# Second block: projections of unnormalised tokens ahead of the norm's root, and attention scores read from banks of their own

## The reference

```
mod = split(silu(c) @ w_mod + b_mod, 6)      # shift1, scale1, gate1, shift2, scale2, gate2: vectors
xn  = rms_norm(x, g1) * (1 + scale1) + shift1
p   = xn @ w_in                              # queries, keys, values, Fourier, convolution, pool
x   = x + gate1 * (concat(attention, fourier, conv, pool) @ w_out)
xn  = rms_norm(x, g2) * (1 + scale2) + shift2
x   = x + gate2 * ((silu(xn @ w_a) * (xn @ w_g)) @ w_ffn_out)
```

## Time and profile before

| | us |
|---|---|
| median of three runs | 2863.41 |
| span of the profiled execution, first to last instruction | 2801.5 |
| around the span (median less span) | 61.9 |
| TensorE busy in the span | 2548.0 |
| VectorE, ScalarE, GpSimd busy | 1445.6, 908.4, 1104.0 |

### The profile page before, as it was taken

How to read it: one execution, slowest core, us unless ns; L and a number is a source line. 1 busy time by engine, 2 the same in 40 slices (tenths; PEclk the granted TensorE clock), 3 DMA queues, 4 the chain that set the end, 5 groups by cost and what they waited for, 6 DMA issues and landing times.

```text
span 2801.5 us, 29890 instructions
## 1 busy us (share of the span) xinstructions
PE 2548.0 (91%) x9872; PEld 1720.8 (61%) x9872; DVE 1445.6 (52%) x3086; ACT 908.4 (32%) x2255; POOL 1104.0 (39%) x1163
## 2 busy tenths in 40 slices
PE   7899899987988888998998889998887999979999
PEld 6567655433434455686555546574365888857888
DVE  1732776898877436316767767777545100161000
ACT  1242254445553322422444445423333100132000
POOL 0000576676777600003776666766634000070000
PEclk9999999999999999999999999999998999989999
DMA  6465899999999963658999999999931344413444
GB/s 249 150 255 185 352 420 421 420 420 381 407 420 420 420 260 135 248 189 316 420 420 420 420 420 402 420 421 420 421 138 60 135 151 150 143 68 112 155 153 150
DMA packets 187329, 817.52 MB, mean 292 GB/s; under 512 B 20608, under 2 KB 22688, under 8 KB 154160
## 3 DMA queue, kind: packets, MB, share of 16 engines
q0 software_dynamic: 148816, 549.32, 48.1%
q1 hardware_dynamic: 38368, 266.35, 25.7%
HBM read 814.54 MB, written 1.05 MB: 291 GB/s over the span
## 4 chain that ended last, share of the span: by engine, by line
PE 50%; DMA 18%; POOL 13%; DVE 11%; issue 6%; ACT 1%; SPq 0%; ACTq 0%; DVEq 0%; POOLq 0%
PE work L642 42%; DMA arena<-experts_down,arena 10%; PE acc L642 7%; DMA arena<-experts_up,arena 7%; POOL arena L583 6%; POOL arena L610 6%; DVE arena L1754 3%; DVE arena L1669 1%; DMA ring<-stream 1%; DVE small L1592 1%; PE work L716 1%; DVE arena L1592 1%; DVE mx L1604 1%; DVE arena L1603 0%; DVE arena L1930 0%
## 5 line engine op out<-in xcount | busy, mean ns | idle before, releaser
L642 PE MATMUL acc<-arena 128*128 128x512 f32 x1868 | 892.7, 614 | 151.6 <-DMA arena<-experts_up,arena 106.9
L610 POOL DMA_INDIRECT arena<-experts_down,arena x512 | 495.6, 968 | 811.0 <-DVE arena L1738 570.7
L1754 DVE SCALAR_TENSOR_TENSOR arena<-arena,acc 128x1024 f32<-128x1024 f32 x512 | 619.1, 1220 | 329.6 <-DMA arena<-experts_down,arena 315.2
L642 PE MATMUL work<-arena,ring 128*128 128x256 f32 x3460 | 760.0, 382 | 19.5 <-ACT arena L1522 14.5
L642 PEld LDWEIGHTS work<-arena,ring 128*128 128x128 f32 x3460 | 660.8, 191 | 122.1 <-issue 24.6
L642 PEld LDWEIGHTS acc<-arena 128*128 128x128 f32 x1868 | 346.8, 194 | 602.3 <-issue 469.4
L583 POOL DMA_INDIRECT arena<-experts_up,arena x512 | 493.3, 963 | 199.9 <-issue 147.1
L642 PE MATMUL work<-h,ring 128*128 128x256 f32 (+1 forms) x1504 | 339.5, 380 | 8.4 <-DMA ring<-stream 6.0
L642 PEld LDWEIGHTS work<-h,ring 128*128 128x128 f32 x1504 | 279.5, 194 | 75.7 <-issue 40.1
L1310 ACT ACTIVATE arena<-arena 128x2 f32<-128x2 f32 x256 | 52.0, 203 | 598.8 <-DVE arena L1754 392.6
L642 PE MATMUL work<-lent,ring 128*128 128x256 f32 x992 | 224.3, 379 | 0.0
(11 more groups left out here) (241 smaller groups left out, 1833.5 us busy)
## 6 DMA issues: line engine op xcount, KB each, us to landing
ring<-stream SPq DMA_DIRECT2D x252, 1024.0 KB, 4.9
arena<-experts_down,arena POOLq DMA_INDIRECT x512, 14.7
arena<-experts_up,arena POOLq DMA_INDIRECT x512, 14.8
arena<-na_bias POOLq DMA_DIRECT2D x2, 2048.0 KB, 14.5
arena<-consts POOLq DMA_DIRECT2D x1, 2392.0 KB, 20.2
lent<-consts POOLq DMA_DIRECT2D x2, 1024.0 KB, 16.3
arena<-consts POOLq DMA_DIRECT2D x1, 1816.0 KB, 19.3
x<-x_in SPq DMA_DIRECT2D x1, 1024.0 KB, 5.7
```

The source lines that it names most:

```text
L610: pool.indirect_dma_start(down[:, (l * PICKS + n) % ROWS, :], None, experts[2 * l], bass.IndirectOffsetOnAxis(ap=expert[:, n:n + 1], axis=0))\
L642: ins = nc.tensor.matmul(o, w, r, start=start, stop=stop, **kw)
L1754: ins = v.scalar_tensor_tensor(row, row, 1.0, tok, ALU.mult, ALU.mult, accum_out=dot[:, n:n + 1])
```

## The change

Since the root is one factor for each token, it can be multiplied in behind a projection as well as ahead of it. The change does so for two of the projections behind each of the four norms. VectorE makes a second set of tiles, `gx2`: `x1` by the column `gs`, and beside the 256 tokens a 257th column that holds the shift. TensorE multiplies one projection of `gx2` ahead of the square sums and one behind them; in the result the first 256 columns want the root yet, and the 257th is the projected shift. VectorE reads that out (`scale_raw`): the column to `raw_bias`, the rest by the reciprocal root. Ahead of the mixers these are the two projections `a` of the convolution (ScalarE's copies of them are gone), ahead of the feed-forward the pair of the first hidden tile.

The square sums take three products instead of eight: VectorE adds the squares of the first six tiles (`add_square`), the last two go to TensorE as they are. The normalised tiles are now `gx2` by the reciprocal root. The scaling stands in `add_gated` behind each residual tile; in the first layer's first norm it stands by itself.

In the attention of the second block the scores go to the four banks of `acc` and not to `work`; VectorE takes the maximum there, ScalarE reads them there for the exponential, with the scale in it, and the pass L1603 is gone. TensorE waits, from the third pair on, for the exponentials of two pairs earlier. A number of semaphores of the first block, one for each layer before, become one for both with counts that go on; the order of work there stays. In the diff these lines are left out.

```diff
-            if kind in "STO":
+            if kind in "TO" or kind == "S" and beside:
...
+        gx2 = carve(KD, T + 2)
+        raw_bias = carve(2, 1)
...
+        def score_bank(u):
+            return acc[:, (u % 4) * 2 * T:(u % 4 + 1) * 2 * T]
...
+                    if kind == "S" and not beside:
+                        if p >= 2:
+                            pe.wait_ge(sem(f"{name}_exp"), pair[1] - 3)
+                        for u in pair:
+                            mm(score_bank(u), units[u]["q"][0], units[u]["k"], inc=sem("scored2"))
...
-                square_sum(f"norm2_{l}", f"sq2_{l}", k1("ones_d"), lambda k: h2[:, k, :], KD, T, 1)
-                for i in range(N_FM2):
+                def raw_group(item, norm):
+
+                    b = bank(item)
+                    for k in range(KD):
+                        w = tile()
+                        pe.wait_ge(sem("gx2"), (norm - 1) * KD + k + 1)
+                        mm(b[:, 0:T + 1], w, gx2[:, k, 0:T + 1], k == 0, k == KD - 1,
+                           inc=bank_full if k == KD - 1 else None)
+                        read()
...
+                def sum_of_squares(item, ready, norm):
+
+                    b = bank(item)
+                    pe.wait_ge(sem("sq_part2"), norm)
+                    mm(b[:, 0:T], k1("ones_d"), sq_part2, True, False)
+                    for k in (KD - 2, KD - 1):
+                        pe.wait_ge(sem(ready), k + 1)
+                        mm(b[:, 0:T], k1("ones_d"), h2[:, k, :], False, k == KD - 1,
+                           inc=bank_full if k == KD - 1 else None)
+
+                raw_group(f"fm{l}", 2 * l + 1)
+                sum_of_squares(f"norm2_{l}", f"sq2_{l}", 2 * l + 1)
+                raw_next(f"fm{l}")
+                for i in range(2, N_FM2):
...
-                square_sum(f"fnorm2_{l}", f"sqf2_{l}", k1("ones_d"), lambda k: h2[:, k, :], KD, T, 1)
-                for j in range(2 * KF):
+                raw_group(f"ffn{l}", 2 * l + 2)
+                sum_of_squares(f"fnorm2_{l}", f"sqf2_{l}", 2 * l + 2)
+                raw_next(f"ffn{l}")
+                for j in range(2, 2 * KF):
...
+                    if not beside:
+                        A.step(f(prob_[:, s, :], score_bank(u), ACT.Exp, bias=neg_mx[:, s, 0:1], scale=SCALE,
+                                 accum_out=total[:, s, 0:1]), f"{name}_exp")
+                        return
...
+                copied(act, f"ffn{l}", 0)
+                A.step(f(silu_a[:, 0, :], silu_a[:, 0, :], ACT.Silu, bias=raw_bias[:, 0, :]), "ffn_silu")
...
+                    if un["bias"] is None:
+                        V.need("scored2", l * len(units) + u + 1)
+                        V.step(v.tensor_reduce(mx[:, s, 0:1], score_bank(u), AX.X, ALU.max))
+                        V.step(v.tensor_scalar(neg_mx[:, s, 0:1], mx[:, s, 0:1], -SCALE, None, ALU.mult), f"{name}_score")
+                        return
...
+                def scale_tokens(k, gs):
+                    V.step(v.tensor_scalar(gx2[:, k, 0:T], x1[:, k, :], gs[:, k:k + 1], None, ALU.mult), "gx2", last=False)
+
+                def add_square(k, squares):
+
+                    V.need(squares, k + 1)
+                    V.step(v.tensor_tensor(sq_part2, h2[:, 0, :] if k == 1 else sq_part2, h2[:, k, :], ALU.add),
+                           "sq_part2" if k == KD - 3 else None)
+
+                def normalise_tokens(item, norm, done):
                     copied(dve, item, 0)
                     V.step(v.reciprocal(rnorm2, rnorm2))
+                    V.need("gx2", norm * KD)
                     for k in range(KD):
-                        V.step(stt(h2[:, k, :], x1[:, k, :], gs[:, k:k + 1], rnorm2), done, last=False)
...
+                        V.step(v.tensor_tensor(h2[:, k, :], gx2[:, k, 0:T], rnorm2, ALU.mult), done, last=False)
+
+                def scale_raw(o, item, j):
+
+                    b = V.full(item, j)
+                    V.step(v.tensor_copy(raw_bias[:, j, :], b[:, T:T + 1]))
+                    V.free(v.tensor_tensor(o, b[:, 0:T], rnorm2, ALU.mult), item, j)
...
+                        if squares:
+                            scale_tokens(n, gs)
+                            if 2 <= n < KD - 1:
+                                add_square(n - 1, squares)
```

More of the change, by code:

```diff
@@ L1105, in _, with raw_next @@
             for l in range(DEPTH):
-                square_sum(f"norm2_{l}", f"sq2_{l}", k1("ones_d"), lambda k: h2[:, k, :], KD, T, 1)
-                for i in range(N_FM2):
+                def raw_group(item, norm):
[6 more added lines that the diff above has]
+                        read()
+                def raw_next(item):
+                    b = bank(item, 1)
+                    for k in range(KD):
+                        mm(b[:, 0:T + 1], tile(), gx2[:, k, 0:T + 1], k == 0, k == KD - 1,
+                           inc=bank_full if k == KD - 1 else None)
+                        read()
+                def sum_of_squares(item, ready, norm):
[5 more added lines that the diff above has]
+                        mm(b[:, 0:T], k1("ones_d"), h2[:, k, :], False, k == KD - 1,
+                           inc=bank_full if k == KD - 1 else None)
+                raw_group(f"fm{l}", 2 * l + 1)
+                sum_of_squares(f"norm2_{l}", f"sq2_{l}", 2 * l + 1)
+                raw_next(f"fm{l}")
+                for i in range(2, N_FM2):
                     if i == NORMS_AFTER:
@@ L1190, in _ @@
                     for k in range(KF):
-                        if n == 0:
+                        if n == 0 and k == 0:
+                            pe.wait_ge(sem("hid_raw"), l + 1)
+                        elif n == 0:
                             copied(pe, f"ffn{l}", 2 * k + 1)
@@ L1578, in _ @@
                 shift(f"hsf2_{l}", f"hf2_{l}", 3)
-                for j in range(KF):
+                copied(act, f"ffn{l}", 0)
+                A.step(f(silu_a[:, 0, :], silu_a[:, 0, :], ACT.Silu, bias=raw_bias[:, 0, :]), "ffn_silu")
+                for j in range(1, KF):
                     b = A.full(f"ffn{l}", 2 * j)
-                    if j >= 2:
+                    if j == 2:
+                        A.need("hid_raw", l + 1)
+                    elif j > 2:
                         copied(act, f"ffn{l}", 2 * (j - 2) + 1)
@@ L1748, in dots @@
                 def dots(q):
-                    V.need(f"tok{l}", q // TILE_GROUPS + 1)
+                    V.need("tok", l * TT + q // TILE_GROUPS + 1)
                     for n in range(q * GROUP, (q + 1) * GROUP):
@@ new lines, in scale_raw @@
+                def scale_raw(o, item, j):
+                    b = V.full(item, j)
+                    V.step(v.tensor_copy(raw_bias[:, j, :], b[:, T:T + 1]))
+                    V.free(v.tensor_tensor(o, b[:, 0:T], rnorm2, ALU.mult), item, j)
+                if l == 0:
+                    shift_column(0)
+                    for k in range(KD):
+                        scale_tokens(k, gs1)
+                    for k in range(1, KD - 2):
+                        add_square(k, f"sq2_{l}")
+                normalise_tokens(f"norm2_{l}", 2 * l + 1, f"hs2_{l}")
@@ L1935, in _ @@
+                for n in range(2):
+                    scale_raw(ca[:, n, :], f"fm{l}", n)
                 V.need("zeroed", 3)
@@ L1994, in _ @@
                            f"ffn{l}", 2 * j + 1)
-                add_gated(f"ffo{l}", 5)
+                if l + 1 < DEPTH:
+                    following = mods[:, l + 1, :, :]
+                    for gs, g, chunk in ((gs1, "g1", 1), (gs2, "g2", 4)):
+                        V.step(stt(gs.unsqueeze(2), following[:, chunk * KD:(chunk + 1) * KD, 1:2], 1.0,
+                                   k2(g, l + 1).unsqueeze(2), ALU.add, ALU.mult))
+                    V.step(v.tensor_copy(gx2[:, :, T:T + 1], following[:, 0:KD, 1:2]))
+                    add_gated(f"ffo{l}", 5, gs1, f"sq2_{l + 1}")
+                else:
+                    add_gated(f"ffo{l}", 5)
 def tiles_of(w, order):
```

80 lines of the change are left out of this document (42 added, 38 removed).

## The result

| kernel | median, us | range, runs | ratio to before on the same chip, 95% interval |
|---|---|---|---|
| before | 2865.15 | 2862.77 to 2868.02, 4 | |
| after | 2831.57 | 2828.18 to 2836.59, 4 | 0.988 [0.9868, 0.9892] |

What follows compares the result with a forecast made beforehand. TensorE, busy 91% of the span, was taken as the bound, with time to win in its stalls, lower clock and removable work. Norms 27.7 plus attention 5.0 gave 32.7 us less: 2801.5 - 32.7 + 61.9 = 2830.7 us, range 2823 to 2843.

Steps and rivals of the forecast that it cites:

- The norms: Four norms of the second block: filled stalls, fewer square products and a kept clock gain 7.6 + 7.6 + 8.8 + 3.7 = 27.7 us.
- the clock: First projection behind three norms: no longer slowed by TensorE's lower clock after the stall, 6.3 us of the gain.
- rival B: Behind the norms: TensorE's clock falls all the same, 6.3 us lost again, 2837.0 us; chance 0.11.
- Layer 0's mixer norm: First norm of the second block: scalings and additions hide behind nothing, so the gain is only 3.7 us.
- The width of 257: Raw projections with the shift as extra column: 0.1 us more; 14 us if priced like width 384.
- The way out: VectorE multiplies raw results by the root, done 2.9 us behind the third projection's start; bank wanted at 3.7, so covered.
- The attention: Attention of both layers: one VectorE pass fewer in each of 16 units, taken as 2.5 us a layer, 5.0.
- The bound from GpSimd: End of both attentions: GpSimd's convolution taps cap the gain at about 3.0 and 5.3 us, 8.3 together.
- rival C: Attention: it gives all that GpSimd's taps allow, 8.3 us, for 2827.4 us; chance 0.08.
- Reading the scores where they lie: Attention: VectorE's maximum from PSUM costs what it cost from SBUF, 691 for 686 ns; the skill's figures would add 1.0 us.
- Rivals A and D: A: attention gives nothing, 2835.7 us, chance 0.16. D: its lower clock lasts into the next stage, 2886.5 us, chance 0.03.
- The frame: Whole kernel: profiled span of 2801.5 us plus an untouched 61.9 us around it makes the median of 2863.4.

Runs made afterwards that it cites:

- raw_ahead: The changed kernel with both raw projections ahead of the square sums, leaving nothing to fill the root's time; 2861.97 us, ratio to before 0.9950.
- dummy_fill: The kernel before with seven useless products of constants behind each norm's square sums, while TensorE waits for the root; 2855.79 us, ratio to before 0.9962.
- old_scores_gate: The changed kernel with the old attention (shared score banks, VectorE scaling pass) and the convolution's two gate projections swapped; 2850.50 us, ratio to before 0.9915.
- pass_kept: The changed kernel with the convolution's gate projections swapped and VectorE's scaling pass back, scores still in their own banks; 2848.18 us, ratio to before 0.9897.
- after_again: The changed kernel, unedited, run once more beside before on another chip; 2830.42 us, ratio to before 0.9871.
- attn_only: The kernel before with only the attention part of the change; 2871.11 us, ratio to before 0.9975.
- gate_swapped: The changed kernel with the convolution's two gate projections swapped, so GpSimd's half is ready first; 2824.67 us, ratio to before 0.9847.
- sums_only: The kernel before with the square sums cut from eight products to three, VectorE adding squares, nothing else; 2866.48 us, ratio to before 0.9994.

## Why the prediction was right, point by point

**The norms.** They were forecast at 27.7 us. To the start of the third projection the prediction's own marks give 16.19 to 8.44 us in layer 0's feed-forward (forecast 8.4 behind the last output projection), 16.19 to 8.44 in layer 1's, 17.39 to 8.40 in layer 1's mixers and 14.52 to 11.32 in layer 0's: 7.75, 7.75, 8.99 and 3.20, together 27.7 as well. But these marks are not alike. For before the prediction took the moment at which the second projection is read (2202.96) for the start of the third; TensorE's own record of the third stands at 2202.69, 0.27 us earlier. With the same marks in both traces, the readers of the seventh feed-forward projection among them (the first row is of before, the second of after), the second block falls into these stretches:

```profile
2220.20 0.38 ACT L1583 ACTIVATE arena<-work 128x256 f32<-128x256 f32 x1 [6.52 <-PE work L642]
...
2267.89 0.38 ACT L1635 ACTIVATE arena<-work 128x256 f32<-128x256 f32 x1 [6.52 <-PE work L648]
```

| stretch of the second block, us | before | after | less |
|---|---|---|---|
| last residual of the first block to the first scores (mixer norm, layer 0) | 55.20 | 52.60 | 2.60 |
| attention stretch, layer 0 | 42.22 | 37.56 | 4.66 |
| to the reader of the seventh feed-forward projection (norm, layer 0) | 66.80 | 59.39 | 7.41 |
| to the first scores of layer 1 (mixer norm, layer 1) | 261.56 | 252.93 | 8.63 |
| attention stretch, layer 1 | 43.82 | 40.73 | 3.09 |
| to the reader of the seventh feed-forward projection (norm, layer 1) | 66.80 | 59.39 | 7.41 |
| to the end of the span | 209.11 | 209.13 | -0.02 |

So the norms gave 26.0 us, not 27.7, and the attention 7.8, not 5.0. The sum of 33.8 is the whole difference of the second blocks, but for rounding, and that it lies so near the forecast's 32.7 is in part luck: the two misses have opposite signs. raw_ahead shows the filling, dummy_fill the clock, with 6.3 us for three norms as forecast; rival B did not come.

**Layer 0's mixer norm** is where most of the norms' miss lies: 2.6 us for 3.7 forecast. Its third projection starts 11.3 us behind the residual for a forecast of 10.6, for another reason than the one I gave. The additions, which I had last, ended at 2123.40, well ahead of the sums at 2124.66. What was late is the raw projection: it waited 2.09 us for the first scaled tile and then began at 1.2 GHz (0.50 up to 2122.00). I took its 3.48 us from rows at 1.00. old_scores_gate, which has the same norm and the same wait of 2.09 us, shows the other case, since its clock stayed at 1.00:

```profile
2131.08 3.71 PE L648 MATMUL work<-arena,ring 128*128 128x257 f32 x16 [2.09 <-DVE arena L1976]
...
2135.09 1.53 PE L648 MATMUL work<-arena,c 128*128 128x256 f32 x6 [0.30 <-DVE arena L1981]
```

There the sums do wait for the additions (L1981; 0.30 us, some 1 us forecast), and the third projection starts at 2140.16, 10.3 us behind the residual's end at 2129.88.

**The width of 257** costs nothing that shows: layer 0's first raw projection of the feed-forward takes 3.48 us, from 2241.86 to the sums at 2245.34, as one of 256 columns does. **The way out** is done at 2252.65 + 0.42, 2.8 us behind the third projection's start (2.9 forecast), and TensorE waits for no bank.

**The attention** was the term that was most off in size: 5.0 forecast, 7.8 measured in this pair of traces (stretches 86.0 to 78.3 us); the means of the five traces with the old scores and the four with the new ones in the old gate order, 85.3 and 78.9, say 6.4. I let half of VectorE's passes count, since TensorE at 0.64 of its clock seemed next to wait. pass_kept shows that, with GpSimd out of the way, all of them counted. The bound from GpSimd (3.0 and 5.3 us) was about right, and was reached: 3.5 and 4.6 us were won at the taps, the traces of after, after_again, attn_only and raw_ahead all wait for the taps, and gate_swapped takes 6.7 us more once the wait is lifted. So the attention went by rival C's mechanism. Behind the taps layer 0 won 1.2 us more, and layer 1 lost 1.5 at the lower clock (2547.64 to 2561.55, 13.9 us, for 12.4 before).

**Reading the scores where they lie** cost what the row said. The timeline of after:

```profile
2174.00 0.69 DVE L1653 TENSOR_REDUCE mx<-acc 128x1 f32<-128x512 f32 x1
...
2175.34 0.69 ACT L1264 ACTIVATE arena<-acc,neg_mx 128x512 f32<-128x512 f32 x1
```

0.69 us for the maximum from PSUM, 0.686 from SBUF. The Trainium skill (VectorE: DVE Perf Modes, the section on the TRN2 errata) gives a PSUM source a larger fixed cost than an SBUF one, 0.065 us more by the prediction's estimate; this trace does not show it.

**Rivals A and D** did not come: the attention gave more, not nothing, and in layer 0 the stage behind it ran at 1.00 from 2199.5 on, as in the earlier trace rows. In layer 1 the lower clock did last on into the first 28 records, at the cost of the 1.5 us above.

**The frame was wrong.** The 61.9 us "around the span" were the difference between the median and an execution that was not like the others. The forecast was saved by being a difference inside one trace, added to a median. Had a term come from the first block, or had I scaled with the span, it would have been off.

## What to carry to other kernels

A stall of the matrix engine is priced with the slow stretch behind it, and what helps is work put into it: taking away work ahead of it only moved the wait here (sums_only: nothing; one projection moved: 20 us). Where one stage gets faster, look up how far ahead its neighbour finishes: here 3 and 5 us of GpSimd's slack capped the gain, and two lines that changed an order lifted it. Compare span and time of the same execution before the difference is called overhead, and compare traces stage by stage rather than by span, between marks that are the same instruction in both.

## What the runs showed of the hardware

- The granted clock behind a stall of the same 3.6 us is not fixed: at layer 0's mixer norm it was 1.00 in one trace of the same kernel and 0.50 in another. Seven products of constants in the stall, 3.19 us of work for nothing, kept it at 1.00 behind all four norms in dummy_fill; by the medians that kernel is 12.8 us faster, and 6.3 to 8.8 us of its trace's gain lie in the norms.
- The same holds ahead of the sums: behind the same wait of 2.09 us the first raw projection of layer 0 ran at 0.50 in after (5.29 us) and at 1.00 in old_scores_gate (3.71 us).
- With the experts' gathers under way the transfers moved 411 GB/s in one execution and 383 in another (400 to 800 us); the first blocks of the two differ by 68 us. Medians of before lay between 2865 and 2876 us on the chips used, so medians are compared on one chip only.
- A load of ScalarE's function table takes 1.28 us. In sums_only it ended last ahead of the root (2251.90, the sums at 2251.35); before, the eight square sums outlasted it (2190.39, the load 2189.27).
- Reading 512 columns from a PSUM bank in place of SBUF changed little: VectorE's maximum took 691 ns for 686, ScalarE's exponential 687 for 722.
